# Latent heads' normalising factors made once, applied by VectorE inside the attention units

## The reference, cut to what matters

```python
def rmsnorm(x, g):
    y = x * lax.rsqrt(jnp.mean(x * x, axis=-1, keepdims=True) + EPS)
    return y * g

def mla_q(cq, g_qa, w_qb, g_q, rope):                    # cq: tokens x 384
    q = jnp.dot(rmsnorm(cq, g_qa), w_qb).reshape(B, T, 8, 96)
    q = rmsnorm(q, g_q)                                  # one factor per head and token
    ... rope on q[..., 64:]

def mla_kv(ckv, k_rope, g_kva, w_kvb, g_k, rope):        # ckv: tokens x 256
    kv = jnp.dot(rmsnorm(ckv, g_kva), w_kvb).reshape(B, T, 8, 128)
    k_nope, v = kv[..., :64], kv[..., 64:]
    k = rmsnorm(jnp.concatenate([k_nope, k_pe], -1), g_k)  # k_pe: k_rope for every head
    ... rope on k[..., 64:]
```

## Time and profile before

| what | value |
|---|---|
| time, median of 3 runs | 2733.93 us (2732.76 to 2734.04) |
| the profiled execution's own time | 2732.19 us |
| its span (first to last instruction) | 2730.4 us |
| PE busy | 2631.9 us (96%) |
| DVE / ACT / POOL busy | 1476.8 / 927.6 / 323.4 us |
| TensorE's mean granted clock | 0.984 of full speed |
| `latent_stage` in the trace | about 172.7 to 270.7 us |
| `attend_stage` in the trace | about 270.9 to 488 us |

### The profile page before, as it was taken

How to read it: one execution, slowest core, us unless ns; L and a number is a source line. 1 busy time by engine, 2 the same in 40 slices (tenths; PEclk the granted TensorE clock), 3 DMA queues, 4 the chain that set the end, 5 groups by cost and what they waited for, 6 DMA issues and landing times. The chain is left out here.

```text
span 2730.4 us, 32399 instructions
## 1 busy us (share of the span) xinstructions
PE 2631.9 (96%) x13360; PEld 2167.5 (79%) x13360; DVE 1476.8 (54%) x2007; ACT 927.6 (34%) x1260; POOL 323.4 (12%) x200
## 2 busy tenths in 40 slices
PE   7998999999999999999899999999998999999998
PEld 5876566788888888889787888887686778888887
DVE  6326775965449345562484643445798824533332
ACT  4332666333212112352363432323323623322221
POOL 2110222000000000000350000000330643000000
PEclk9999999999999999999899999999999999999999
DMA  7011100523226333122001223222210222222221
GB/s 279 25 45 51 43 16 16 187 106 108 93 108 210 112 113 142 65 78 78 18 1 62 108 75 119 83 93 73 100 63 1 93 108 79 89 94 99 100 78 63
DMA packets 37326, 237.16 MB, mean 87 GB/s; under 512 B 4160, under 2 KB 5184, under 8 KB 13504
## 3 DMA queue, kind: packets, MB, share of 16 engines
q1 hardware_dynamic: 37184, 235.15, 24.1%
HBM read 233.04 MB, written 2.10 MB: 86 GB/s over the span
## 5 line engine op out<-in xcount | busy, mean ns | idle before, releaser
L377 PE MATMUL pair<-h_high,w_high 128*128 128x512 f32 x1984 | 715.9, 370 | 6.2 <-POOLq L4033 2.2
L378 PE MATMUL pair<-h_low,w_high 128*128 128x512 f32 x1984 | 712.0, 367 | 0.0
L383 PE MATMUL pair<-h_high,w_low 128*128 128x512 f32 x1984 | 444.4, 367 | 0.0
L331 DVE TENSOR_TENSOR w_low<-ring,w_high 128x2048 fp32r<-128x2048 f32 (+5 forms) x164 | 342.2, 2092 | 178.7 <-ACT w_high L309 171.1
L377 PEld LDWEIGHTS pair<-h_high,w_high 128*128 128x128 f32 x1984 | 374.8, 189 | 72.3 <-issue 5.8
L378 PEld LDWEIGHTS pair<-h_low,w_high 128*128 128x128 f32 x1984 | 375.6, 189 | 63.7 <-issue 1.4
L383 PEld LDWEIGHTS pair<-h_high,w_low 128*128 128x128 f32 x1984 | 346.4, 189 | 61.7
L309 ACT ACTIVATE w_high<-ring 128x2048 fp32r<-128x2048 f32 (+4 forms) x166 | 288.1, 1736 | 304.1 <-PE pair L383 204.0
L377 PE MATMUL pair<-high,w_high 128*128 128x512 f32 (+1 forms) x704 | 249.4, 364 | 0.8 <-DVE low L1320 0.8
L378 PE MATMUL pair<-low,w_high 128*128 128x512 f32 (+1 forms) x704 | 249.3, 364 | 0.0
L319 POOL CAST w_high<-ring 128x1024 fp32r<-128x1024 f32 x25 | 30.6, 1250 | 1261.5 <-DVE coef L732 703.7
(11 more groups left out here) (491 smaller groups left out, 3957.3 us busy)
## 6 DMA issues: line engine op xcount, KB each, us to landing
ring<-in_w_up SPq DMA_DIRECT2D x66, 1024.0 KB, 4.8
ring<-in_w_ada SPq DMA_DIRECT2D x32, 1024.0 KB, 4.9
ring<-in_w_down SPq DMA_DIRECT2D x32, 704.0 KB, 4.0
ring<-in_w_ada0r SPq DMA_DIRECT2D x16, 1024.0 KB, 4.8
ring<-in_w_merge_b SPq DMA_DIRECT2D x14, 1024.0 KB, 4.8
ring<-in_w_down SPq DMA_DIRECT2D x8, 1024.0 KB, 4.7
ring<-in_w_att_in SPq DMA_DIRECT2D x6, 1024.0 KB, 4.8
ring<-in_w_heads SPq DMA_DIRECT2D x6, 1024.0 KB, 4.9
```

What stands on the lines that cost most here:

```text
L331: (on or self.nc.vector).tensor_tensor(self.w_low[:, n % 2, 0:floats], self.ring[:, chunk % RING, 0:floats], self.w_high[:, n % 2, 0:float ...
L377: self.nc.tensor.matmul(out[:, a:e], w_high[:, k, at], high[:, k, a:e], start=k == 0, stop=False)
L378: self.nc.tensor.matmul(out[:, a:e], w_high[:, k, at], low[:, k, a:e], start=False, stop=False)
L383: mm = self.nc.tensor.matmul(out[:, a:e], w_low[:, k, at], high[:, k, a:e], start=False, stop=k == kt - 1)
```

## The change

The factors are no longer spread by PE and applied in `latent_stage`. One accumulation in `stat` now holds the sums of squares of all 16 heads (rows 0 to 7 queries, 8 to 15 keys; the selecting matrices get 8 more columns). At its end ACT makes all factors at once, as exp(-0.5 ln(x)), in `low[:, 2]` (two instructions instead of two roots and DVE's two long reciprocals). The rotary features are put in place unscaled: 8 copies on DVE for the queries, 8 on POOL for the keys. The eight `bring_back`s, 32 `finish` instructions, the load of `back` and two of the three groups of idle products (14 and 18 of 46; the last 14 stay) go. The six one-column sums of `rkv` move from the middle to the stage's begin. The values use three bank pairs in turn and are all scaled by DVE.

In `attend_stage` ACT issues two transfers in each of units 0 to 7, right after the unit's first exponential: one row of 768 factors (3 KB, one partition) to 96 partitions each, in one of three buffers. From the fourth on, each first waits until the multiplication of the buffer's former content is done. At the end of its iteration, after `join_max`, DVE waits for each and multiplies it into one head's `kT` or `qT` (two `finish(n)` in each of units 0 to 7). `stage_plain` and `take_lat(8)` wait for them. `top` becomes a tensor of its own, since `c_high[:, 4]` is now a buffer.

```diff
@@ attend_stage
+        top = stack.enter_context(K.temp("top", [P, 2, 6], F32R))
+        rows = mixT[:, 2, :]
+        factor = [mixT[:, 3, :], c_high[:, 4, :].bitcast(F32), c_low[:, 4, :].bitcast(F32)]
@@ ACT
+            def load_factor(n):
+                if n >= 3:
+                    act.wait_ge(finished.sem, finished.base + n - 2)
+                row = n // 2 if n % 2 else 8 + n // 2
+                act.dma_start(factor[n % 3][0:96, :], rows[row:row + 1, :].unsqueeze(1).broadcast_to([1, 96, ALL])).then_inc(
+                    factor_loaded[n % 3].sem, 16)
             def stage_plain(u):
+                act.wait_ge(finished.sem, finished.base + 2 * (u - 8) + 2)
@@ take_lat
+                if u == 8:
+                    act.wait_ge(finished.sem, finished.base + 16)
@@ after the exponential of each step
+                    if s == 0 and gqa(u):
+                        load_factor(2 * u)
+                        load_factor(2 * u + 1)
@@ DVE
+            def finish(n):
+                h, to = n // 2, qT if n % 2 else kT
+                dve.wait_ge(factor_loaded[n % 3].sem, factor_loaded[n % 3].base + 16 * (n // 3 + 1))
+                nc.vector.tensor_tensor(to[:, h, :], to[:, h, :], factor[n % 3][0:96, :],
+                                        ALU.mult).then_inc(finished.sem, 1)
@@ DVE, after join_max(u + 1)
+                if gqa(u):
+                    finish(2 * u)
+                    finish(2 * u + 1)
@@ latent_stage
-    inv_q, inv_k = low[:, 4, :], low[:, 2, :]
+    factors = low[:, 2, :]
+    values_of = lambda t: K.pairs[(3, 0, 1)[t % 3]]
@@ PE, at the begin
+            for t in range(6):
+                mm = nc.tensor.matmul(K.pairs[1][:, t:t + 1], csq[:, 1, t * P:t * P + P], K.ones[:, 0:1], start=True, stop=True)
+            mm.then_inc(spread.sem, 1)
             raw(0)
+            pe.wait_ge(rooted.sem, rooted.base + 2)
             raw(1)
@@ PE, from the last rotation on
             rotate(2)
-            K.keep_busy(side[:, 512:], 14)
-            ... (the six one-column sums, their wait)
-            pe.wait_ge(rooted.sem, rooted.base + 2)
-            add_sums(sel_ckv, csq[:, 1, :], start=True)
+            add_sums(sel_ckv, csq[:, 1, :])
             ...
             sums(8)
-            ... (bring_back and values in turn, two keep_busy)
+            values(0)
+            values(1)
             sums(9)
+            for t in range(2, 6):
+                values(t)
+            pe.wait_ge(dve_valued.sem, dve_valued.base + 4)
             for t in range(6):
+                mm = nc.tensor.matmul(side[:, t * P:t * P + P], K.xT[:, 7, t * P:t * P + P], K.ident[:],
+                                      start=True, stop=True)
             K.keep_busy(K.psum[:, 512:], 14)
@@ ACT
+            nc.scalar.activation(factors, stat[:, 0:ALL], ACT.Ln, bias=K.eps2[:], scale=1.0 / 96).then_inc(rooted.sem, 1)
+            act.wait_ge(rooted.sem, rooted.base + 3)
+            nc.scalar.activation(factors, factors, ACT.Exp, scale=-0.5).then_inc(rooted.sem, 1)
@@ DVE
             sines(2)
-            ... (finish x8 with two instructions for each head, two reciprocals of 128x768)
+            dve.wait_ge(rotated.sem, rotated.base + 2)
+            for h in range(8):
+                nc.vector.tensor_copy(qT[64:96, h, :], rope(h // 4)[32 * (h % 4):32 * (h % 4) + 32, :])
             K.split_low(dve, fv)
             K.split_low(dve, fv + 1)
+            dve.wait_ge(inverted.sem, inverted.base + 1)
+            for t in range(6):
+                scale_values(t)
@@ POOL
+            pool.wait_ge(rotated.sem, rotated.base + 3)
+            for h in range(8):
+                chain.step(nc.gpsimd.tensor_copy(kT[64:96, h, :], rope(2)[64:96, :]))
+            chain.sync()
```

More of the change, by code:

```diff
@@ L168, in __init__ @@
         self.constants_loaded = sem("constants_loaded")
+        self.factor_loaded = [sem(f"factor_loaded{n}") for n in range(3)]
         self.pe_a = sem("pe_a")
@@ L2705, in rotate @@
                 nc.tensor.matmul(side[:, 0:LAT], rotm[:], rope(n)[:, 0:LAT], start=True, stop=True).then_inc(spread.sem, 1)
[L2707 to L2710, removed]
             def values(t):
[L2713 to L2717, removed]
+                if t == 0:
+                    side_free(4)
+                elif t < 3:
+                    pe.wait_ge(squared.sem, squared.base + 9 + t)
                 else:
-                    pe.wait_ge(dve_valued.sem, dve_valued.base + t // 2)
+                    pe.wait_ge(dve_valued.sem, dve_valued.base + t - 2)
                 at = slice(t * P, t * P + P)
@@ L2824, in _ @@
             root(side[:, 0:ALL], side[:, 0:ALL], 1.0 / CTX, K.eps)
+            act.wait_ge(spread.sem, spread.base + 2)
+            root(rkv[:], K.pairs[1][:, 0:6], 1.0 / CTX, K.eps)
             nc.scalar.activation(ident_r[:], K.ident[:], ACT.Copy)
@@ L2852, in _ @@
             act.wait_ge(summed.sem, summed.base + 13)
[L2853 to L2857, removed]
+            nc.scalar.activation(factors, stat[:, 0:ALL], ACT.Ln, bias=K.eps2[:], scale=1.0 / 96).then_inc(rooted.sem, 1)
+            act.wait_ge(rooted.sem, rooted.base + 3)
+            nc.scalar.activation(factors, factors, ACT.Exp, scale=-0.5).then_inc(rooted.sem, 1)
             act.wait_ge(valued.sem, valued.base + 7)
             act.wait_ge(rotated.sem, rotated.base + 3)
[L2861 to L2864, removed]
+            of = side[:, 0:ALL].rearrange("p (t h c) -> p h t c", h=2, c=64)
+            nc.scalar.activation(val[:, 4:6, :, 0:64], of, ACT.Copy).then_inc(act_valued.sem, 1)
+            act.wait_ge(act_valued.sem, act_valued.base + 1)
             nc.scalar.activation(val[:, 4:6, :, 128:192], val[:, 4:6, :, 0:64], ACT.Copy)
@@ L2868, in _ @@
         def _(dve):
-            chain = Chain(dve, K.dve_chain)
             def sines(n):
-                dve.wait_ge(spread.sem, spread.base + 2 + n)
+                dve.wait_ge(spread.sem, spread.base + 3 + n)
                 if n > 0:
@@ L2876, in sines @@
                 else:
-                    dve.wait_ge(K.loaded.sem, K.loaded.base + 64)
+                    dve.wait_ge(K.loaded.sem, K.loaded.base + 48)
                 nc.vector.tensor_tensor(ys, side[:, 0:LAT], trig[:, 1, :], ALU.mult).then_inc(consumed.sem, 1)
[L2880 to L2892, removed]
             def scale_values(t):
@@ L2902, in _ @@
             nc.vector.tensor_tensor(low[:, 5, :], low[:, 5, :], side[:, 0:ALL], ALU.mult).then_inc(consumed.sem, 1)
+            dve.wait_ge(rooted.sem, rooted.base + 2)
+            nc.vector.reciprocal(rkv[:], rkv[:]).then_inc(inverted.sem, 1)
             K.split_low(dve, fq + 2)
@@ L2935, in _ @@
             nc.gpsimd.memset(val[:, 0:4, :, 64:128].rearrange("p g t c -> p (g t) c"), 1.0)
-            pool.wait_ge(K.loaded.sem, K.loaded.base + 64)
+            pool.wait_ge(K.loaded.sem, K.loaded.base + 48)
             for n in range(3):
-                pool.wait_ge(spread.sem, spread.base + 2 + n)
+                pool.wait_ge(spread.sem, spread.base + 3 + n)
                 y = rope(n)[:, 0:LAT]
@@ L2948, in _ @@
             chain.close()
-    K.loaded.base += 64
-    for c, n in ((raw_done, 10), (summed, 13), (spread, 13), (valued, 7), (read, 10), (squared, 11), (rooted, 4),
-                 (kr_ready, 1), (act_valued, 5), (consumed, 13), (inverted, 3), (dve_valued, 3), (rotated, 3)):
+    K.loaded.base += 48
+    for c, n in ((raw_done, 10), (summed, 13), (spread, 5), (valued, 7), (read, 10), (squared, 11), (rooted, 4),
+                 (kr_ready, 1), (act_valued, 1), (consumed, 4), (inverted, 1), (dve_valued, 6), (rotated, 3)):
         c.base += n
@@ L4401, in lay_out @@
     out["sel2"], out["back"] = two, back
-    out["sel"] = np.concatenate([two, four, heads8 * np.float32(EPS * 96 / 384), heads8 * np.float32(EPS * 96 / 256), heads8], 1)
+    keys8 = np.roll(heads8, 8, 1)
+    wide = np.concatenate([zeros(P, 8), two], 1)
+    out["sel"] = np.concatenate([wide, four, heads8 * np.float32(EPS * 96 / 384), keys8 * np.float32(EPS * 96 / 256), keys8], 1)
     out["ones64"] = np.kron(np.eye(2), np.ones((64, 64))).astype(np.float32)
```

71 lines of the change are left out of this document (11 added, 60 removed).

## The result

| kernel | us, median (lowest to highest) | ratio to before, 95% interval |
|---|---|---|
| before | 2733.35 (2732.06 to 2734.04), 4 runs | |
| after | 2752.21 (2750.98 to 2754.14), 4 runs | 1.0071 (1.0056 to 1.0087) |

The change costs 18.9 us. The forecast was slower by 52. The direction and the cause (the source of the transfers limits them) are the forecast's; the size is not, because the transfers did not run one behind the other. The profiled execution of after took 2754.14 us, 22.0 more than that of before; 1.8 of these lie ahead of the changed stage, which begins at 174.5 instead of 172.7 us. That start lies anywhere between 172.2 and 175.4 us in the traces of this document's kernels, so these 1.8 us are scatter.

A forecast was written before the change was run, and what follows sets the result against it. The prediction took DVE to bound the latent stage's tail and PE the units; 33 us saved there, counted against 16 back-to-back transfers of 11.2 us, left +51.8 us, so 2786 us, range 2697 to 2820.

The forecast's parts named there:

- What bounds it: Before the change, DVE bounds the latent stage's tail and PE the eight grouped-head units after it.
- The latent stage: Latent stage ends at 237.6, attention begins at 237.9 instead of 270.99: 33 us saved (bounds 30 and 36).
- DVE's and ACT's added work in the units: Units 0 to 7: two multiplications and two issues each cost 0.5 us a unit, 4 us (bounds 1 and 10).
- The clock: After units 0 to 7, PE's granted clock may start low once, costing 1 us.
- The source limits, at the rate of one sixteenth: Units' transfers: one source partition gives a sixteenth of 423 GB/s, 26.4 GB/s, so 11.2 us a transfer.
- that a partition has one way out: Unproved assumption behind 11.2 us a transfer: a partition's rate is the same whichever engine asks.
- So the 16 transfers run back to back: Units 0 to 7: the queue stays full, so the transfers take 16 x 11.2 = 179.2 us.
- So the last lands: Last transfer lands at 432.5; DVE's work follows until 439.0, shifting PE's fourth peak piece for unit 9 by 51.8 us.
- the likeliest case: Transfers in the units take 11 to 13 us each; 2786 us, own range 2768 to 2818, chance 0.57.
- rival 2: In between: 6 to 9 us a transfer in the units, break-even about 8.0, giving 2710 to 2750; chance 0.07.
- rival 1: The source does not limit: transfers land in 2 to 5 us, 2705 us (2696 to 2715); chance 0.31.
- What would show it: Landings of 11 us growing to 20, DVE waits of 8 to 20 us a unit, units of 22.4, attention at 238.

The follow-up runs named there:

- e4: The changed kernel without its 16 transfers and without its 16 multiplications in the attention units: 2699.06 us, 0.9875 of before.
- e1: The changed kernel without transfers; DVE still multiplies, by the tile that holds the factors, and waits for nothing: 2699.19 us, 0.9878 of before.
- e2: The changed kernel with the same 16 transfers of 288 KB, each read from 96 partitions instead of one: 2698.34 us, 0.9875 of before.
- g0: The changed kernel with every transfer reading the same partition 0: 2780.48 us, 1.0177 of before.
- e5: The changed kernel with each transfer reading four neighbouring partitions, 0 to 3, 24 times each: 2794.59 us, 1.0223 of before.
- g1: The changed kernel with keys' transfers reading partition 0 and queries' partition 1: 2780.29 us, 1.0178 of before.
- g4: The changed kernel with keys' transfers reading partition 0 and queries' partition 4: 2753.57 us, 1.0081 of before.
- f1: The changed kernel with each head's sum in 8 partitions 16 apart, each read 12 times per transfer; whole computation: 2702.42 us, 0.9890 of before.
- h1: The changed kernel with the 16 factor rows stored once to HBM and read from there; whole computation: 2701.68 us, 0.9886 of before.
- e3: The changed kernel with each transfer writing 48 partitions instead of 96, still from one partition; multiplications cover 48: 2702.05 us, 0.9891 of before.

## Why the prediction was right and wrong

- **What bounds it**: right. PE in the units, DVE in the stage's tail; the tail went, and e4 has the gain.
- **The latent stage**, forecast 33 us saved, attention at 237.9: 34.1 in the trace, 33.7 by e4, attention at 238.7. DVE's and POOL's copies do take turns: 1.13 us each for DVE instead of 0.55 while POOL's 8 run beside them (215.04 to 223.91), through at 222.0, as written. The Trainium skill's rule on the two engines ("SBUF — State Buffer", Who interferes with whom) agrees. The wait that this caused was 0.6 us and not 3, since PE came to the values at 222.7 and not at 219.8 (1.8 of it from ahead of the stage); the start, 223.4, is just past the 222 to 223 written. Two small slips in the sum changed nothing: 0.415 us for 512 elements makes 0.62 for 768 by length, not 0.55, and 270.99 to 237.9 is 33.1, not the 33.3 that the first exponential was moved by.
- **DVE's and ACT's added work in the units**, forecast 4 us "if the transfers arrive in time": nothing measurable (e1 and e2 against e4). DVE's spare time held both multiplications.
- **The clock**, forecast to start low once behind these units, 1 us: it was at 1.00 there (404.2 to 480), but at 0.50 in a part of each of the four odd units, which the sum did not have. PE was busy 114.0 us with the eight units' work instead of 96.2; how much of that cost the kernel time no run separates.
- **The source limits, at the rate of one sixteenth**: right. 11.2 us a transfer forecast at 26.4 GB/s; 10.8 measured at 27.2 where they queue (g0), 12.4 from issue to landing for one alone. The assumption "that a partition has one way out" was too narrow: four neighbours share it (e5, g1).
- **"So the 16 transfers run back to back"**: this step failed, and it is the size of the error. The sum had 16 x 11.2 = 179.2 us (with 1.9 fixed, 181) between the first issue and the last landing; in after it is 146, from 251.4 to 397.5. That is 35 us less, and the shift is 33 smaller than forecast (18.9 against 51.8). Two things stand in its place. Transfers of different groups overlap: the 16 occupied the queue for 126 us, 7.9 each. g0, where all read one group, is what the forecast described, and took 2780.5; g4 differs from g0 in nothing but that every second transfer reads partition 4, and is 27 us faster. And the queue was not always full: it stood empty for 4.4, 7.2 and 7.9 us after every fourth landing, about 20 us, since DVE's maxima after a late factor hold back the next unit, at whose first exponential ACT issues.
- **"So the last lands", then 6.5 us of DVE's work**: with the queue no longer full, this path is gone too. The last multiplication (402.35) does not wait for the last landing (397.5). The path runs through the second landing of each pair of units, about 22 us, and DVE's and PE's work behind it, about 16, four times. That 35 and 33 lie so near is therefore in part chance. I put the rows' partition numbers nowhere into the sum, though the diff shows them (`row = n // 2 if n % 2 else 8 + n // 2`), and what I quoted of the port rule in the prediction was its rate alone.
- **The range** (2697 to 2820) has the time inside, but the likeliest case's own range (2768 to 2818) does not. The time fell between that and rival 2 (2710 to 2750, chance 0.07), so it is inside the stated range only because that was drawn from rival 1 to the forecast: luck. Rival 2's reckoning comes near: 7.9 us a transfer would be at the break-even of 8.0 if the queue were full, and the gaps of 20 make the 19 us.
- **What would show it**: landings of 12.4 growing to 21.9 and copies in turn came as written, and attention's first idle products at 238.7, for 238. DVE's waits of 8 to 9 us a unit came in every second one. Units of 22.4 did not come: there were pairs of 12.4 and 26.

## What to carry to other kernels

A row that is to be spread over partitions by a transfer is read once for each copy: count the bytes read from each group of neighbouring source partitions, not only those written, at 27 GB/s a group. Put copies of the row in several groups (f1: free, as the selecting matrix had empty columns), or go through HBM (h1, where the same transfer falls from 12.4 to 3.8 us); both gave 30 us. And where a sum says "one after the other", look at which resource each of the transfers uses before multiplying: here the choice of the rows alone was worth 27 us (g0 against g4).

## What the runs showed that was not expected

- ACT's issue of a transfer, 0.5 to 0.6 us in general, takes 4.8 to 5.8 us for every fourth transfer of after (265.66 above), when two others are still under way, and up to 5.5 in g0, 5.9 in g1 and 4.2 in e5; ACT's exponentials are queued behind it, and PE waits for these (`ACT c_low L2169 <- issue` and `PE pair L2116 <- ACT prob` above). In after each of these issues ended 2.7 to 3.5 us before the landing that DVE was waiting for. In f1, h1 and e2, where transfers land early, no issue takes over 1.3. What blocks it was not tested. The forecast's 0.7 to 0.9 a unit did not have it.
- In after the second of two transfers issued together lands 9.2 to 10.1 us after the first although they read different groups, little less than the 10.9 of g0; the large overlap begins with the third. In e3, with half the reads, it begins with the second (2.5 to 3.2 us). What decides this stays open. So does the difference between 12.0 us (e5) and 10.8 (g0): the fewer reads under way in e5 may be the reason, but no run separates them from the place.
- A group share was tested for partitions 0 to 3 against 4 (and 8, 12), no others.
